# Attention: other row tables that set the order of scores, turns and value products on TensorE and of takes and lows on VectorE

## The reference, cut to what matters

```
for blk in range(S // Q_BLOCK):                      # 16 blocks of 128 queries
    s = einsum("bhqd,bhkd->bhqk", q[blk], k[:q1])    # scores against all keys up to q1
    s = s + cum[q] - cum[k]                          # forget gates
    p = softmax(where(causal, s, -inf))
    outs.append(einsum("bhqk,bhkd->bhqd", p, v[:q1]))
o = concatenate(outs) ; return (o * silu(gate)) @ w_out
```

## Time and profile before

| what | us |
|---|---|
| median of 3 runs (lowest, highest) | 2367.14 (2367.10, 2368.56) |
| the profiled execution, its own time | 2368.27 |
| its span, first to last instruction | 2366.5 |
| busy in the span: PE / PEld | 2337.6 / 2023.0 |
| busy in the span: DVE / ACT / POOL | 1345.9 / 1108.3 / 618.5 |
| granted TensorE clock, mean | 0.996 of full |
| first takes of head 0 / head 1 / head 2 | 739.27 / 780.46 / 829.91 |

### The profile page before, as it was taken

The page is one execution under the profiler, slowest core; times in us unless marked ns, Lnnn a source line. Parts: engine busy times, 40 slices in busy tenths (PEclk is TensorE's granted clock), DMA queues, the critical chain, the costliest instruction groups (busy, mean ns, idle before and its releaser), DMA issues. The chain is left out here.

```text
span 2366.5 us, 36441 instructions
## 1 busy us (share of the span) xinstructions
PE 2337.6 (99%) x13373; PEld 2023.0 (85%) x13373; DVE 1345.9 (57%) x2772; ACT 1108.3 (47%) x2060; POOL 618.5 (26%) x718
## 2 busy tenths in 40 slices
PE   9999999999999999999999999999999999999998
PEld 7888889999887999889999899778888888887887
DVE  4221121241014998999989999836535565667733
ACT  3111111221114888888888888812024565657300
POOL 0000000000000465655666556516420000000354
PEclk9999999999999999999999999999999999999999
DMA  6444443342126455565555665385623354448572
GB/s 208 142 124 115 125 116 108 109 138 93 67 84 161 99 121 116 133 144 135 120 116 132 144 138 120 89 264 157 206 93 123 118 165 133 134 136 307 190 241 97
DMA packets 221305, 328.77 MB, mean 139 GB/s; under 512 B 17468, under 2 KB 144764, under 8 KB 215308
## 3 DMA queue, kind: packets, MB, share of 16 engines
q1 hardware_dynamic: 220616, 325.91, 48.5%
q0 software_dynamic: 512, 0.53, 0.1%
HBM read 199.89 MB, written 126.48 MB: 138 GB/s over the span
## 5 line engine op out<-in xcount | busy, mean ns | idle before, releaser
L990 DVE TENSOR_TENSOR at_pl<-at_tps,at_ph 128x512 fp32r<-128x512 f32 (+3 forms) x640 | 371.9, 604 | 14.2 <-ACT at_ph L913 14.1
L913 ACT ACTIVATE at_ph<-at_tps 128x512 fp32r<-128x512 f32 (+3 forms) x640 | 306.4, 535 | 102.6 <-PE at_ops L842 72.0
L380 ACT ACTIVATE pa_stg<-pa_ps 128x512 fp32r<-128x512 f32 (+1 forms) x120 | 71.8, 598 | 575.4 <-PE pa_ps L272 569.4
L822 PE MATMUL at_tps<-ident,at_probs 128*128 128x128 f32 x2176 | 329.7, 274 | 1.6 <-DVE at_pl L990 1.2
L842 PE MATMUL at_ops<-at_ph,at_val 128*128 128x256 f32 (+1 forms) x1152 | 325.9, 303 | 1.7 <-DVE at_pl L990 1.7
L903 ACT ACTIVATE at_probs<-at_probs,at_least 128x128 f32<-128x128 f32 (+15 forms) x256 | 308.8, 1206 | 0.0
L272 PE MATMUL pa_ps<-pa_xh,pa_wh 128*128 128x512 f32 x760 | 298.8, 393 | 0.0
L842 PE MATMUL at_ops<-at_pl,at_val 128*128 128x256 f32 (+1 forms) x1152 | 298.1, 282 | 0.0
L272 PE MATMUL pa_ps<-pa_xh,pa_wl 128*128 128x512 f32 x760 | 297.3, 391 | 0.0
L272 PE MATMUL pa_ps<-pa_xl,pa_wh 128*128 128x512 f32 x760 | 296.9, 391 | 0.0
L822 PEld LDWEIGHTS at_tps<-ident,at_probs 128*128 128x128 f32 x2176 | 254.5, 141 | 34.2 <-DVE at_pl L990 10.9
(11 more groups left out here) (203 smaller groups left out, 4518.3 us busy)
## 6 DMA issues: line engine op xcount, KB each, us to landing
at_q<-q_halves SPq DMA_DIRECT2D x45, 512.0 KB
at_k<-k_halves SPq DMA_DIRECT2D x45, 512.0 KB
q_halves<-pa_stg SPq DMA_DIRECT2D x32, 512.0 KB, 3.7
k_halves<-pa_stg SPq DMA_DIRECT2D x32, 512.0 KB, 3.7
v_halves<-pa_stg SPq DMA_DIRECT2D x32, 512.0 KB, 3.1
y_gated<-re_work SPq DMA_DIRECT2D x32, 512.0 KB, 2.9
at_val<-v_halves SPq DMA_DIRECT2D x15, 1024.0 KB, 17.4
pa_wst<-in_attn_w_in SPq DMA_DIRECT2D x14, 1024.0 KB, 7.1
```

Of the source, the lines that this page charges most:

```text
L380: nc.scalar.activation(out, source(kind, s), func, scale=scale).then_inc(evac_h, 1)
L822: mm = nc.tensor.transpose(tps[c % TB][:, k, :], probs[s % ROWS][:, t0:t0 + P], ident[:, :])
L913: nc.scalar.activation(ph[g % 2][:, j * PB:j * PB + n, i % 2 * P:(i % 2 + 1) * P], tps[c % TB][:, 0:n, :], ACT.Copy).then_inc(high_out, 1)
L990: nc.vector.tensor_tensor(pl[g % 2][at], tps[c % TB][:, 0:n, :], raw(ph[g % 2][at]), ALU.subtract)\
```

## The change

Only the two tables change; the letters of each kind are as many as before (40 S, 40 T and 72 V on PE; 40 X and 40 L on DVE), and so are all instructions.

```diff
-    TENSOR_ROWS = ("VTTVTVTSVVVT", "S", "STTVVTVVVVTVTTVVTV", "SV", "STVVVVVVTVSVVVVTVVV", "SVVVVVS", "SVTS",
...
+    TENSOR_ROWS = ("TVTTSVTVV", "SVTVTTV", "SVVTVTVVTVTTVVVT", "SVVT", "SVVTVSV", "SVSVVVV", "SVVVVVSVVVVT",
+                   "STVSTV", "STVSTSVTV", "SVSTTSVV", "STSVTVSVV", "STTSTVSVVVT", "SVVTSTTSVVTSVV", "SSVVTVSVVST",
...
-    VECTOR_ROWS = ("LXLLLL", "XLLL", "XLLLL", "X", "XLX", "XLX", "XLX", "XLX", "XLXLXLL", "XXLXL", "XXLX", "XLXXL",
-                   "XLXXLLX", "XLLXLXLXL", "XLXLXLXL", "XXLLXLX")
+    VECTOR_ROWS = ("LLLLXL", "XLLLL", "XLL", "XL", "XX", "XLLX", "XXL", "XLX", "XLXLXL", "XLXLX", "XLXLXL",
+                   "XLXLXLL", "XLXLXXL", "XLXXLX", "XLXLXLX", "XLXLLXLX")
```

More of the change, by code:

```diff
@@ L543, in attend @@
     PB = BANK // P
-    TENSOR_ROWS = ("VTTVTVTSVVVT", "S", "STTVVTVVVVTVTTVVTV", "SV", "STVVVVVVTVSVVVVTVVV", "SVVVVVS", "SVTS",
-                   "STVTS", "STVVSTVSTV", "STSVTTSV", "SVSTTS", "SVVTSVSTVV", "SVSTVSTVVVSV", "STTSSTVVVVTSVT",
-                   "STVSVTSVTVVST", "SVVTSVVVVSS")
-    VECTOR_ROWS = ("LXLLLL", "XLLL", "XLLLL", "X", "XLX", "XLX", "XLX", "XLX", "XLXLXLL", "XXLXL", "XXLX", "XLXXL",
-                   "XLXXLLX", "XLLXLXLXL", "XLXLXLXL", "XXLLXLX")
+    TENSOR_ROWS = ("TVTTSVTVV", "SVTVTTV", "SVVTVTVVTVTTVVVT", "SVVT", "SVVTVSV", "SVSVVVV", "SVVVVVSVVVVT",
+                   "STVSTV", "STVSTSVTV", "SVSTTSVV", "STSVTVSVV", "STTSTVSVVVT", "SVVTSTTSVVTSVV", "SSVVTVSVVST",
+                   "SVTSTSVSTVT", "SVVVSVTSVVS")
+    VECTOR_ROWS = ("LLLLXL", "XLLLL", "XLL", "XL", "XX", "XLLX", "XXL", "XLX", "XLXLXL", "XLXLX", "XLXLXL",
+                   "XLXLXLL", "XLXLXXL", "XLXXLX", "XLXLXLX", "XLXLLXLX")
     n_chunks = [(s % QT) // PB + 1 for s in range(STEPS)]
```

## The result

The changed kernel takes 2406.97 us (median of 4, 2405.79 to 2408.17), the kernel before 2367.85 in the same job: a ratio of 1.0164, 95% interval 1.0151 to 1.0177, or 39.1 us slower. The sign was predicted, the size was not: 2390 was forecast and 2402 was the end of the range. The profiled execution took 2405.8 with a span of 2404.0 (2366.5 before); the clock was 0.996 in both.

A forecast was written before the change was run, and what follows sets the result against it. PE's work was taken to bound the attention: 48.5 us a head plus waits of 1.0 and 1.4 and 0.1 for loads make 51.0, 1.5 more than before. Over 15 heads that adds 22.5 us: 2390 us, range 2368 to 2402.

The forecast's parts named there:

- What bounds the kernel: Attention stage: PE's work bounds it, 48.5 of 49.5 us a head, with about 1.0 us of waits.
- First trip: V(6, 13) to T(2, 0): PE waits for H(0, 0) and E(2) on ACT, 1.0 us a head.
- Second trip: V(7, 15) to T(7, 0): PE's 6.86 us of work falls short of ACT's 8.19 us chain, costing 1.4 us.
- Exposed loads: PE's weight loads not prefetched behind a wait: 0.1 us a head.
- The old waits on DVE should go: PE's waits on DVE, 1.0 us a head, vanish as DVE catches up and is needed less in rows 9 to 15.
- sign of being wrong: Old waits of scores on takes still 0.5 us a head would show the prediction wrong.
- After that PE has more to do than ACT's chain needs: Behind T(7, 0): E(10) and later are done well before their turns, so no further wait was booked.
- Both trips, and the old waits stay: Rival: DVE is late again in rows 9 to 15; +2.3 us a head, 2402 us; chance 0.12.
- The faster ones: Two rivals: evened scores without binding trips, 2355 us, chance 0.08; only the loads' 45.0 us counting, 2335, chance 0.02.
- only the first trip: Rival: the wait at T(2, 0) alone costs, ACT's chain behind V(7, 15) being covered; 2368 us, chance 0.10.
- Fewer successions: DVE's direct successions of takes: at most 0.1 us a head overall, booked as nothing; 0.5 less work in rows 9 to 15.
- The sum: Attention: PE's work, two waits and exposed loads make 51.0 us a head, 1.5 more, over 15 heads 22.5 us.

The follow-up runs named there:

- r2: Changed kernel with ACT doing the exponential ahead of the high parts at row numbers 3 and 5 only: 2377.64 us.
- r3: Changed kernel with T(2, 0) moved later in TensorE's table, behind V(7, 0), S(4, 1), V(7, 1) and S(5, 0): 2393.79 us.
- r12: Changed kernel with take X(12, 0) put ahead of low L(9, 0) in VectorE's rows 11 and 12: 2400.75 us, ratio 1.0147.
- r9: Changed kernel with VectorE's row 12 as XLXLXLX, a low between X(12, 2) and X(12, 3): 2410.67 us.
- r14: Changed kernel with exponentials first at row numbers 3 and 5, T(12, 3) earlier, X(12, 0) ahead of L(9, 0), X(9, 1) ahead of L(5, 1): 2373.31 us.
- r5: Changed kernel with T(12, 3) moved earlier in TensorE's row 15, directly behind S(15, 0): 2401.18 us.
- r10: Kernel before with three direct successions of takes taken apart in VectorE's rows 11, 12 and 15: 2368.69 us, ratio 1.0009.
- r1: VectorE's new table paired with TensorE's table of before: 2464.61 us.
- r13: Changed kernel with exponentials first at row numbers 3 and 5, T(12, 3) earlier in row 15, X(12, 0) ahead of L(9, 0): 2368.52 us, ratio 1.0003.

## Why the prediction was right in direction and too low

- **What bounds the kernel**: right in kind. A head is PE's work and its waits, and every edit moved a head by what it did to PE's waits. The split was slightly off: 49.52 less 1.27 of waits is 48.25 of work, where 48.5 and 1.0 were summed.
- **First trip**: right, 1.01 against 1.0 us. r2 and r3 show the cause.
- **Second trip**: the chain was right (8.18 against 8.19 us). PE's work in it was mis-sized: from 1163.85 to 1172.08 are 8.23 us, less 1.15 of waits 7.08, where 6.86 was summed; some 0.11 of it is the loads exposed behind T(4, 0) and T(5, 0). So 1.15 instead of 1.4.
- **Exposed loads**: "0.1 for weight loads that are not prefetched behind a wait" had no row behind it. Measured are 0.3: about 0.057 us with each of the four waits on exponentials and 0.07 with that of T(15, 0).
- **The step that failed** is "The old waits on DVE should go". Booked as 1.0 us off a head, they gave back 0.42; 0.85 us a head stayed, which is more than the 0.5 that the prediction itself named as a sign of being wrong. DVE does catch up in the waits of rows 2 to 7, but in row 11 it stands before L(9, 0), which waits for ACT, with a take that is ready behind it; r12 moves that take ahead of it and 0.23 us a head return. The cause of the rest, 0.6 us before scores of rows 8 to 14, stays open: r9 and r14 show only that a take put elsewhere there costs more than it gives.
- **What was left out**, and is the second step that failed, is the third trip. "After that PE has more to do than ACT's chain needs" was worked out for E(10) and later as turns wait for them, not for the place where a turn waits for a low, a low for an H, and that H for ACT's chain behind T(12, 3). It cost 0.47 and 0.07 of load (r5).
- **The rivals**: the nearest is "Both trips, and the old waits stay", at 2402. It came near in size, but not by its mechanism: in r2, where E(4) no longer waits and T(2, 0) does not either, the scores of rows 10 to 14 wait as long as before, so these trips do not make them late. The faster ones and "only the first trip" are excluded by the waits on L903. "Fewer successions" was worth nothing, as booked for DVE's work as a whole; but the gain that it was to bring in rows 9 to 15 was not found: in r9 and r10 taking more of them apart cost 0.27 and 0.13 us a head.
- **The sum** with the measured sizes: 49.52 - 1.27 + 0.85 + 1.01 + 1.15 + 0.47 + 0.3 = 52.03 us a head, against 52.06. Against the 51.0 of the prediction, the waits of scores that stayed make +0.85, the third trip +0.47 and the loads +0.2; the second trip and PE's own work, both 0.25 smaller than summed, take 0.5 off. That the miss was not larger is luck in these two.

## What to carry to other kernels

When an order of one engine is changed, walk every in-order queue of the others from each wait that the move makes tighter to the first instruction that needs what stands behind, through buffers that must come free as well as through data; the prediction did that for two of three places. A wait that the order removes elsewhere is gained only if its own producer is not held up later: look in the trace for an instruction that waits with a ready one behind it. Two tables that are tuned together must be costed together, since one alone (r1) lost 6.4 us a head.

## What the runs showed that was not expected

- A wait on PE costs more than the wait: behind each of the four waits on exponentials the second transpose starts 0.057 us late, and at most scores that wait the second matmul comes 0.08 to 0.11 us late (0.10 at S(13, 0)), at some, such as S(10, 1) of the changed kernel, only 0.02.
- Two takes in succession cost DVE 0.2 us and can still be the better order, since PE gets the second take's bank 0.4 us earlier (r9, r10). Two of one row that follow each other directly start 0.81 to 0.89 us apart, where a low behind the same take starts 0.61 to 0.67 behind it.
- Reciprocals between two takes do use the wait, as the prediction had it. In the kernel before, row 9, they start 0.61 us behind X(9, 0) (at 1149.40), and X(9, 1) 0.82 behind it, no later than with nothing between:

```profile
1148.79 0.68 DVE L982 TENSOR_SCALAR_CACHE_REDUCE at_probs<-at_sps 128x512 f32<-128x512 f32 x1
...
1149.61 0.75 DVE L982 TENSOR_SCALAR_CACHE_REDUCE at_probs<-at_sps,at_least 128x512 f32<-128x512 f32 x1
```

In the changed kernel, r9, r12 and r13 they start 0.79 us behind X(9, 0), and that is ACT again: they need E(7), whose read ends at 1172.03 in the changed kernel, and start at 1172.06. It is the same in r14 (1153.95 and 1153.99), where X(9, 1) follows 0.12 us behind them:

```profile
1153.99 0.20 DVE L1007 RECIPROCAL at_rden<-at_den 128x8 f32<-128x8 f32 x1
```
